# Tile 0's norm in halves, indices of eight rows first, eleven expert pieces ahead, and a new order of block sums, folds and output projections

## The chip, the cores and the metric

One core of one Trainium2 chip runs the whole program as one launch. The metric is device time in microseconds (us) from the first to the last instruction with what lies around it, as the median of the runs. Five engines work side by side, each through its own list in order: TensorE (PE, and PEld for its weight loads), VectorE (DVE), ScalarE (ACT), GpSimd (POOL) and SyncE (SP). SP and POOL also start the transfers, which share 16 DMA engines. All of the data is float32.

## The reference

256 tokens of width 1024 go through a first block of two layers and then a second block. What bears on the change:

```python
for layer in range(DEPTH):                                    # first block, DEPTH = 2
    mod = c_act @ ada_w[layer] + ada_b[layer]
    sh1, sc1, g1, sh2, sc2, g2 = split(mod, 6)
    h = rms_norm(x, norm_mix_g[layer]) * (1.0 + sc1) + sh1
    y = mlstm_moba_mixer(h, ...) if layer == 0 else diff_attention_mixer(h, ...)   # ends in y @ w_out
    x = x + g1 * y
    h = rms_norm(x, norm_ffn_g[layer]) * (1.0 + sc2) + sh2
    x = x + g2 * peer_ffn(h, peer_wq[layer], peer_keys[layer], peer_u[layer], peer_v[layer])
# peer_ffn: 8 heads, per token and head the top 16 of two lists of 128 sub-keys, the top 16 of the
# 256 pairs, softmax gates; each picked expert e adds gate * v[e] * gelu(u[e] . h)
# second block: three kinds of attention, then 32 experts in 4 groups, two for a token
x = x + concat([out_na, out_dil, out_mem]) @ w_out
x = x + hierarchical_moe(rms_norm(x, g_ffn), w_r1, b_r1, w_r2, b_r2, w1, w3, w2)
```

## The kernel before

Tokens lie in two tiles of 128 partitions (tile 0 and tile 1). The order of each engine is written out by hand; semaphores tie the engines together.

**First layer's mixer.** Weights of 2 MB (`w_slots`) stream through a ring of four places (`ring`, places 0 to 3). Places 0 and 1 take the input projection (`in0`) and the output projection (`out0`, two halves of 512 columns: `first_out` in place 1, `second_out` in place 0); places 2 and 3 take the 20 blocks of `ada_w` (`vec`, `mix`). VectorE weighs a `vec` block by the condition (`weigh(i)`) and TensorE sums it over the partitions with one product ("block sum", `project("vec", ...)`); the four `mix` blocks TensorE multiplies itself, and two of them are folded by one more product each (`fold_blocks`). A place is free when its block is weighed or its groups are multiplied (`slot_free`). Two banks of PSUM (`gp`) take all of these groups in turn: group g waits until group g-2 was copied out, nearly always by ScalarE (`move`). The list `order` numbers the groups, and the counters `gemm_done` and `gemm_moved` count them.

**Towards the retrieval.** After the attention TensorE ends `out0` for tile 0 (L1394), turns the sub-keys (`turn_keys`), multiplies `out0` for tile 1, first half (L1102), turns the normed rows, multiplies query head 0 (`first_query(0)`, L1514) and its scores (L1542), and so on to head 4; the second half of `out0` for tile 1 comes after query 1. Meanwhile VectorE adds the residual of tile 0 and norms it over its full width (`first_residual`, `sum_of_squares`, `first_norm`), then picks the best 16 of head 0 (`topk`, stages 0 to 7; stage 6 puts out the 16 indices, `idx_ready`).

**Rows of the retrieval.** 512 gathers of 1 MB (`PICKS`, L1033 on POOL) bring, for a tile and head, one expert's u and v row to each token. Row n goes to buffer n % 8; `ROW_HOMES` says in which eighth of the ring that buffer lies (homes 0 and 1 are place 0, homes 2 and 3 place 1, and so on). The first eight gathers wait for the place to be free of its weights (`slot_free`; home 4 waits for query 4), every later one for the sum of the row eight before (`vsum`, TensorE, L1555). Of each row VectorE takes the dot product with h (L3091), ScalarE makes the weight, TensorE sums the v part. The other matrix work of both layers and the second block's tile 0 is set between these rows.

**End.** When row 509 has landed SP loads the second block's weights (`in2`, `out2`) into the four places, in the order `turns_of["last"]`, each when its two row buffers are summed (`rows_left`). After the attention come the experts: 8 quads of 4 experts, each quad in 12 pieces of 2 MB (`moe_pieces`; 8 up, 4 down). The first `AHEAD` = 10 pieces have a home before the experts begin, two of them in scattered free rows (`BITS`, pieces 8 and 9); later pieces go through six places, each when TensorE has used the piece before it (`p_used`).

## Time and profile before

| | us |
|---|---|
| median of 3 runs | 2309.93 (2307.38 to 2312.25) |
| profiled execution | 2313.35 |
| its span | 2311.6 |
| PE busy | 1791.5 (77%) |
| DVE busy | 1297.5 (56%) |
| ACT busy | 851.6 (37%) |
| POOL busy | 651.6 (28%) |

The profiled execution is 3.42 us above the median of the runs, and 1.75 us of its time lie outside its span. Views speak of the time from the span's start. A stretch's DMA share is the mean busy share of the 16 DMA engines in it; PEclk is the clock granted to TensorE, as a share of 2.4 GHz. A chain of waits is followed back from the last instruction: each piece released the one behind it, or stood before it on the same engine.

### The profile page before, as it was taken

How to read it: one execution, taken by the hardware profiler on the slowest of the kernel's cores; microseconds unless marked ns; L12 is line 12 of the kernel's file. 1: busy time of each engine (PE TensorE's matmuls, PEld its weight loads, DVE VectorE, ACT ScalarE, POOL GpSimd, SP SyncE). 2: the span in 40 equal slices, each digit the busy share in tenths (PEclk: the TensorE clock that was granted, in tenths of full speed). 3: DMA queues.
4: the chain of work that ended last, by engine and by line, in shares of the span. 5: the costliest groups of instructions: out<-in, count | busy, mean ns of one | idle time of the engine just before them, and what ended most of it. 6: DMA issues, size and time to landing. Idle time of an engine off the chain costs nothing.

```text
span 2311.6 us, 30859 instructions
## 1 busy us (share of the span) xinstructions
PE 1791.5 (77%) x11196; PEld 849.1 (37%) x11196; DVE 1297.5 (56%) x3201; ACT 851.6 (37%) x2294; POOL 651.6 (28%) x606
## 2 busy tenths in 40 slices
PE   9998877695797777588779667777779997666676
PEld 4554531161252343153336112343327552222222
DVE  4877887668757766866875868465442321111111
ACT  1324354444545544454744435444433420000000
POOL 1002344434333443433443444333322300000000
PEclk9999987697798787789979666888979998787878
DMA  9989799999999999999999999999998399999998
GB/s 376 387 340 374 286 409 421 421 419 419 398 421 421 418 421 421 421 390 421 421 421 420 421 420 420 421 417 419 418 387 290 143 387 425 430 427 430 428 428 373
DMA packets 110861, 920.48 MB, mean 398 GB/s; under 512 B 12774, under 2 KB 14852, under 8 KB 18756
## 3 DMA queue, kind: packets, MB, share of 16 engines
q0 software_dynamic: 76800, 549.70, 57.8%
q1 hardware_dynamic: 33924, 369.02, 38.6%
q8 instruction: 77, 1.26, 0.2%
q14 instruction: 60, 0.49, 0.1%
HBM read 917.57 MB, written 6.06 MB: 400 GB/s over the span
## 4 chain that ended last, share of the span: by engine, by line
DMA 45%; PE 36%; DVE 9%; ACT 6%; issue 3%; POOL 1%; DVEq 0%; SPq 0%; POOLq 0%
DMA arena<-in_peer_uv_dram,arena 25%; DMA arena<-in_moe_pieces_dram 14%; PE summed L1555 8%; DVE y_g L3091 4%; PE gp L1102 4%; PE gp L1647 3%; DMA arena<-in_w_parts_dram 3%; PE gp L1116 2%; PE gp L1964 2%; DMA mod<-in_w_parts_dram 2%; PE gp L1107 2%; PE gp L1643 2%; PE gp L1776 1%; ACT arena L2308 1%; PE gp L1527 1%
## 5 line engine op out<-in xcount | busy, mean ns | idle before, releaser
L1555 PE MATMUL summed<-arena 64*64 64x512 f32 x4096 | 690.0, 767 | 338.5 <-ACT arena L2308 314.4
L3091 DVE CUSTOM_DVE_ANT_0 y_g<-arena,h 128x1024 f32<-128x1024 f32 x512 | 627.2, 1225 | 387.1 <-DMA arena<-in_peer_uv_dram,arena 329.3
L1033 POOL DMA_INDIRECT arena<-in_peer_uv_dram,arena x512 | 585.3, 1143 | 890.3 <-PE summed L1555 808.8
L1555 PEld LDWEIGHTS summed<-arena 64*64 64x64 f32 x4096 | 135.8, 157 | 757.3 <-ACT arena L2308 658.4
L2302 ACT ACTIVATE arena<-arena 128x1 f32<-128x1 f32 x512 | 102.5, 200 | 548.6 <-DVE arena L3091 547.5
L1964 PE MATMUL gp<-arena,mod 128*32 128x512 f32 x1008 | 161.4, 778 | 98.8 <-DMA arena<-in_moe_pieces_dram 98.8
L2308 ACT ACTIVATE arena<-cst,arena 128x128 f32<-128x128 f32 x512 | 205.6, 401 | 16.8
L3483 DVE TENSOR_TENSOR mod<-mod,gp 128x512 f32<-128x512 f32 x8 | 5.5, 688 | 357.8 <-ACT mod L2617 357.8
L2305 ACT ACTIVATE arena<-arena 128x1 f32<-128x1 f32 x512 | 150.8, 294 | 16.6
L1964 PEld LDWEIGHTS gp<-arena,mod 128*32 128x32 f32 x1008 | 32.1, 127 | 220.6 <-DMA arena<-in_moe_pieces_dram 160.1
L2617 ACT ACTIVATE mod<-gp 128x512 f32<-128x512 f32 x8 | 4.8, 597 | 252.2 <-PE gp L1964 252.2
L1102 PE MATMUL gp<-arena,hT 128*128 128x512 f32 x208 | 93.0, 604 | 1.2 <-ACT y_g L2090 0.7
L2881 DVE SCALAR_TENSOR_TENSOR h<-arena,cst,h 128x512 f32<-128x512 f32 x98 | 73.9, 754 | 3.4
L2302 ACT ACT_TABLE_LOAD x54 | 69.3, 1283 | 1.0
L1939 PE MATMUL summed<-mod,h 128*128 128x128 f32 x256 | 45.5, 360 | 22.6 <-DVE mod L3478 22.4
L3029 DVE FIND_INDEX8 arena<-arena 128x8 uint32<-128x128 f32 (+1 forms) x192 | 61.8, 330 | 0.0
L3026 DVE MAX8 arena<-arena 128x8 f32<-128x128 f32 (+1 forms) x192 | 58.4, 332 | 4.1 <-ACT arena L2277 0.8
L1102 PEld LDWEIGHTS gp<-arena,hT 128*128 128x128 f32 x208 | 39.4, 193 | 52.8 <-issue 50.3
L2090 ACT ACTIVATE arena<-gp 128x512 f32<-128x512 f32 (+1 forms) x26 | 15.3, 589 | 115.9 <-PE gp L1116 40.2
L2013 PE MATMUL scores<-arena,mod 128*32 128x256 f32 x984 | 56.0, 380 | 1.5 <-DMA arena<-in_moe_pieces_dram 0.8
L1116 PE MATMUL gp<-hT,arena 128*128 128x256 f32 x256 | 56.3, 380 | 0.7 <-ACT hT L2102 0.7
L1647 PE MATMUL gp<-hT,mod 128*128 128x128 f32 x416 | 49.9, 278 | 5.2 <-DMA mod<-in_w_parts_dram 5.2
(521 smaller groups left out, 2333.8 us busy)
## 6 DMA issues: line engine op xcount, KB each, us to landing
arena<-in_moe_pieces_dram SPq DMA_DIRECT2D x93, 2048.0 KB, 25.5
arena<-in_w_slots_dram SPq DMA_DIRECT2D x43, 2048.0 KB, 11.7
arena<-in_w_parts_dram SPq DMA_DIRECT2D x42, 1024.0 KB, 9.4
mod<-in_w_parts_dram SPq DMA_DIRECT2D x23, 1024.0 KB, 9.5
arena<-in_peer_uv_dram,arena POOLq DMA_INDIRECT x512, 15.5
t_rep<-t_rows POOLq DMA_DIRECT2D x1, 3066.0 KB, 18.1
arena<-t_rep POOLq DMA_DIRECT2D x1, 2304.0 KB, 12.7
ext<-in_w_parts_dram SPq DMA_DIRECT2D x2, 1024.0 KB, 16.1
```

The costliest lines, as they stand in the source:

```text
L1033: pool.indirect_dma_start(rowbuf[b], None, a["peer_uv"].rearrange("l n d -> (l n) d"), bass.IndirectOffsetOnAxis(ap=idx[:, col(n):col(n) + ...
L1102: mm = pe.matmul(bank, hT[:, k, grp[1] * P:(grp[1] + 1) * P], w[:, k, :], start=k == 0, stop=k == KT - 1)
L1116: mm = pe.matmul(bank[:, c * S:(c + 1) * S], w[:, k, grp[1] + c * P:grp[1] + (c + 1) * P], hT[:, k, :], start=k == 0, stop=k == KT - 1)
L1555: mm = pe.matmul(op[o:o + HALF, b, :], diag[i:i + HALF, n % DIAGS, i:i + HALF], rowbuf[n % ROWS][i:i + HALF, D + b * 512:D + (b + 1) * 512 ...
L1647: mm = pe.matmul(bank[:, c * P:(c + 1) * P], w[k][:, c * P:(c + 1) * P], hT[:, k, tok], start=k == 0, stop=k == KT - 1)
L1964: mm = pe.matmul(gp[c, j, :], xe[:, 2 * kk + k, c], w[:, e, k, :], start=kk + k == 0, stop=kk == 3 and k == 1, skip_group_check=True)
L2302: link(act.activation(coef[:, c:c + 1], dots[:, c:c + 1], ACT.Gelu))
L2305: link(act.activation(coef[:, c:c + 1], coef[:, c:c + 1], ACT.Copy, scale=gate[:, c:c + 1]))
L2308: act.activation(diag[:, n % DIAGS, :], ident, ACT.Copy, scale=coef[:, c:c + 1]).then_inc(diag_ready, 1)
L2881: ins = v.scalar_tensor_tensor(out=acc, in0=w[:, k, :], scalar=cact[:, k:k + 1], in1=acc, op0=ALU.mult, op1=ALU.add)
L3029: ins = v.max_index(w[:, part], b[:, part], s)
L3091: v.tensor_tensor_reduce(y[:, t, :], rowbuf[n % ROWS][:, 0:D], h[:, t, :], 1.0, 0.0, ALU.mult, ALU.add, dots[:, c:c + 1]).then_inc(udot, 1)
```

## The change

- **Halves.** `first_residual_half(b)` adds tile 0's residual by halves of 512 columns straight out of PSUM (it takes over the two copies that ScalarE made), and takes the squares by halves; `first_norm(0)` writes h by halves, and TensorE turns each half as it comes (`turn_normed`).
- **One factor row.** `scale_norm_rows` multiplies (1 + sc2) into the norm's weight row once, during the mLSTM; `first_norm` then has two passes instead of three, for both tiles.
- **Early indices.** `first_topk` puts out head 0's indices in two parts of eight; POOL waits for the first part at row 0 and for the second at row 8.
- **TensorE's order.** Block sums 8 to 11 and the two folds move from the input projection, the mLSTM and the attention to behind `turn_keys`; the first half of `out0` for tile 1 moves behind query 0's scores, block sum 17 behind query 1, and the second half stands behind query 1's scores. ScalarE's copies move with them. Weighed blocks 8 to 11 and mix parts 6 and 7 now lie in `ext`.
- **Loads.** Query heads 2 and 3 (1 MB each), of which a part lies in `ext`, load when query 0 is multiplied. Head 4 still loads when block 18 is weighed, whose last three steps now stand behind `first_topk`.
- **Homes.** `ROW_HOMES` begins with homes 0 and 1, and `turns_of["last"]` with place 0.
- **Eleven pieces ahead.** Piece 10 of the first quad gets a home: 3584 of 4096 columns in `ext`, loaded behind the last `out2` weights, and 512 columns in `gvec` and `cst`, loaded where the late parts of piece 9 are.

```diff
-ROW_HOMES = (5, 2, 3, 0, 1, 6, 7, 4)
+ROW_HOMES = (0, 1, 2, 3, 5, 6, 7, 4)
-AHEAD = 10
+AHEAD = 11
-VEC_PARTS = ((0, 0), (0, 2), (2, 3), (3, 5), (5, 6), (6, 8), (8, 10), (10, 12))
+VEC_PARTS = ((0, 0), (0, 2), (2, 3), (3, 5), (5, 6), (6, 8), (8, 8), (8, 12))
-        turns_of = dict(..., last=(1, 0, 3, 2, 0, 3, 2, 0, 3, 2))
+        turns_of = dict(..., last=(0, 1, 3, 2, 1, 3, 2, 1, 3, 2))
-        order += [(mix_slots[0], 0)] + [(n, 0) for n in vec_slots[10:12]] + [(n, 0) for n in mix_slots[1:]]
-        order += [(n, 1) for n in mix_slots[2:]]
+        order += [(n, 0) for n in mix_slots]
         first_out, second_out = phase_slots["out0"]
-        order += [(first_out, 0), (second_out, 0), (first_out, 1)]
-        order += [("query", 0), (vec_slots[16], 0), (vec_slots[17], 0), ("query", 1), (second_out, 1), ("query", 2)]
+        order += [(first_out, 0), (second_out, 0)]
+        order += [(n, 0) for n in vec_slots[8:12]] + [(n, 1) for n in mix_slots[2:]]
+        order += [("query", 0), (vec_slots[16], 0), (first_out, 1), ("query", 1), (vec_slots[17], 0), (second_out, 1), ("query", 2)]
...
+                10: (ext[:, 0:14 * S], gvec[:, 0:2 * P], cst[:, C_ROUTE:C_ROUTE + S])}
...
             load_query(1)
-            load_query(2)
...
-            load_query(3)
             for n in range(vec_slots[18], phase_slots["in2"][0]):
                 load_weights(n)
+            sync.wait_ge(gemm_done, group_of["query", 0])
+            load_query(2)
+            load_query(3)
             slot_free(sync, vec_slots[18])
             load_query(4)
...
+            first_bits(10, (0,))
             for n in range(2):
                 sync.wait_ge(gemm_done, group_end(last_held[n]))
                 first_piece(n)
...
             first_bits(9, (1, 2))
+            first_bits(10, (1, 2))
...
-                if n % TOPK == 0:
-                    pool.wait_ge(idx_ready, n // TOPK + 1)
+                if n % TOPK == 0 or n == TOPK // 2:
+                    pool.wait_ge(idx_ready, -(-n // TOPK) + 1 + (n >= TOPK))
...
+            def first_residual_half(b):
...
+                v.tensor_tensor(y[:, 0, c], modrow(2)[:, c], gp[:, g % 2, :], ALU.mult).then_inc(gemm_moved, 1)
+                v.wait_ge(gemm_moved, g + 1)
+                ins = v.tensor_tensor(x[:, 0, c], x[:, 0, c], y[:, 0, c], ALU.add)
...
+                link(v.tensor_tensor_reduce(h[:, 0, c], x[:, 0, c], x[:, 0, c], 1.0, 0.0, ALU.mult, ALU.add, s))
...
+            def scale_norm_rows():
...
+                link(v.scalar_tensor_tensor(out=gvec[:], in0=modrow(4), scalar=1.0, in1=gvec[:], op0=ALU.add, op1=ALU.mult))
...
+            def first_topk():
+
+                for stage in range(3):
+                    topk(0, 0, 0, stage)
+                for r in range(2):
+                    part = slice(8 * r, 8 * r + 8)
+                    if r:
+                        topk(0, 0, 0, 3)
...
+                    pair_rows(part)
+                    pair_hot(part)
+                    pair_index(0, 0, part)
...
-            weigh(17)
-            first_residual(0)
-            sum_of_squares(0)
+            weigh(17, 0, 5)
+            for b in range(2):
+                first_residual_half(b)
...
             first_norm(0)
-            weigh(18)
-            for stage in range(7):
-                topk(0, 0, 0, stage)
+            weigh(17, 5, KT)
+            weigh(18, 0, 5)
+            first_topk()
+            weigh(18, 5, KT)
             weigh(19)
```

TensorE from the end of `out0` for tile 0 to query 2 (rows say line, operation, out<-in, size of the out, count). Before:

```order
L1394 MATMUL gp<-arena,hT 128x512 x8
L1501 MATMUL scores<-cst,arena 128x128 x2
L1102 MATMUL gp<-arena,hT 128x512 x8
L1147 MATMUL turned<-cst,h 128x128 x8
L1514 MATMUL gp<-hT,mod 128x128 x16
L1099 MATMUL gp<-h,ones 128x512
L1542 MATMUL scores<-arena 128x128 x2
L1099 MATMUL gp<-h,ones 128x512
L1514 MATMUL gp<-hT,arena 128x128 x16
L1102 MATMUL gp<-arena,hT 128x512 x8
L1542 MATMUL scores<-arena 128x128 x2
L1514 MATMUL gp<-hT,ext 128x128 x16
```

After:

```order
L1503 MATMUL scores<-cst,arena 128x128 x2
L1103 MATMUL gp<-ext,ones 128x512 x4
L1090 MATMUL gp<-ext,cst 1x512 x2
L1176 MATMUL turned<-cst,h 128x128 x8
L1518 MATMUL gp<-hT,mod 128x128 x16
L1103 MATMUL gp<-h,ones 128x512
L1546 MATMUL scores<-arena 128x128 x2
L1106 MATMUL gp<-arena,hT 128x512 x8
L1518 MATMUL gp<-hT,arena 128x128 x16
L1103 MATMUL gp<-h,ones 128x512
L1546 MATMUL scores<-arena 128x128 x2
L1106 MATMUL gp<-arena,hT 128x512 x8
```

Four block sums and two folds took the place of the first eight L1102 (now L1106), and both halves of that projection stand between query 0 and query 2.

POOL's first gathers with the semaphores that each waits for (`acc_done` counts weighed blocks, `gemm_done` TensorE's groups). Before:

```order
L1033 DMA arena<-in_peer_uv_dram,arena 128x2048 [waits acc_done,idx_ready]
L1033 DMA arena<-in_peer_uv_dram,arena 128x2048 [waits gemm_done] x4
L1033 DMA arena<-in_peer_uv_dram,arena 128x2048 [waits acc_done] x2
L1033 DMA arena<-in_peer_uv_dram,arena 128x2048 [waits gemm_done]
L1033 DMA arena<-in_peer_uv_dram,arena 128x2048 [waits vsum] x8
```

After:

```order
L1037 DMA arena<-in_peer_uv_dram,arena 128x2048 [waits gemm_done,idx_ready]
L1037 DMA arena<-in_peer_uv_dram,arena 128x2048 [waits gemm_done] x3
L1037 DMA arena<-in_peer_uv_dram,arena 128x2048 [waits acc_done] x3
L1037 DMA arena<-in_peer_uv_dram,arena 128x2048 [waits gemm_done]
L1037 DMA arena<-in_peer_uv_dram,arena 128x2048 [waits vsum,idx_ready]
L1037 DMA arena<-in_peer_uv_dram,arena 128x2048 [waits vsum] x7
```

Row 0's gather waited for block 18 to be weighed; now, in place 0, it waits for the last group of `second_out`, which is its tile 1 group.

SP from the second block's last weights to the first piece that waits for `p_used`. After (before, the rows with `ext` and the last `gvec` and `cst` of 256 columns are not there, and the last row has x14):

```order
L808 DMA arena<-in_w_slots_dram 128x4096 [waits gemm_done] x6
L889 DMA ext<-in_moe_pieces_dram 128x3584
L879 DMA arena<-in_moe_pieces_dram 128x4096 [waits gemm_done] x2
...
L889 DMA gvec<-in_moe_pieces_dram 128x768 [waits h_ready,y_ready,r_mm]
L889 DMA cst<-in_moe_pieces_dram 128x768
L889 DMA gvec<-in_moe_pieces_dram 128x256
L889 DMA cst<-in_moe_pieces_dram 128x256
L883 DMA arena<-in_moe_pieces_dram 128x4096 [waits p_used] x13
```

Piece 10's largest part stands ahead of all other pieces and waits for nothing of its own; one piece fewer waits for `p_used`.

## Rows read from the trace of the kernel before

**Rows 1.** The page: span, busy DMA in 40 slices, and the chain by engine.

```profile
span 2311.6 us, 30859 instructions
...
DMA  9989799999999999999999999999998399999998
...
DMA 45%; PE 36%; DVE 9%; ACT 6%; issue 3%; POOL 1%; DVEq 0%; SPq 0%; POOLq 0%
```

**Rows 2.** Stretches: length, busy time by engine, then PEclk, DMA share, GB/s.

```profile
229.00:249.00 20.00, 18.49 (x104) 13.13 (x105) 18.23 (x51) 5.69 (x12) 1.70 (x2) 1.00 0.17 59
249.00:270.00 21.00, 16.84 (x134) 13.23 (x136) 19.36 (x58) 8.72 (x27) 8.96 (x9) 0.92 0.99 394
270.00:276.00 6.00, 6.00 (x57) 3.22 (x50) 3.65 (x8) 4.22 (x9) 4.90 (x4) 1.00 0.91 285
314.00:322.00 8.00, 6.81 (x54) 2.58 (x46) 7.58 (x22) 2.91 (x11) 5.59 (x6) 1.00 0.94 333
322.00:1702.00 1380.00, 1032.74 (x6416) 453.33 (x6412) 941.37 (x2287) 643.71 (x1835) 551.82 (x484) 0.82 1.01 418
1800.00:1833.00 33.00, 29.59 (x226) 19.46 (x224) 14.07 (x76) 21.73 (x52) 17.80 (x18) 1.00 0.01 2
1876.00:1882.00 6.00, 6.00 (x60) 2.04 (x62) 0.16 (x1) 1.88 (x2) 0.00 (x0) 1.00 0.52 165
1882.00:2302.00 420.00, 291.53 (x2300) 118.71 (x2292) 49.43 (x152) 28.90 (x49) 0.00 (x0) 0.83 1.01 428
266.00:268.00 2.00, 2.00 (x12) 0.55 (x12) 1.51 (x7) 1.84 (x8) 0.00 (x0) 0.50 1.01 426
```

**Rows 3.** Chain of waits, 130 to 200 us: start, us, what.

```profile
155.69 1.91 PE gp L1099 x4
...
163.41 10.86 DMA arena<-in_w_slots_dram
...
192.43 0.59 ACT ada_rows L2090
```

**Rows 4.** Chain of waits, 213 to 268 us.

```profile
213.24 7.08 PE gp L1394 x16
...
223.49 1.23 DVE h L3144
...
227.06 1.24 DVE h L3018
...
231.43 3.84 PE gp L1514 x32
235.27 0.86 PE gp L1099 x2
236.13 0.46 PE scores L1542 x4
...
241.42 6.87 PE gp L1102 x16
...
265.75 2.03 PE summed L1555 x8
```

**Rows 5.** VectorE in order of time: start, us, engine, line, what, [idle before].

```profile
177.87 0.42 DVE L2936 TENSOR_TENSOR arena<-cst,turned 128x256 f32<-128x256 f32 x1 [4.65 <-PE turned L1461]
...
246.25 0.17 DVE L3075 TENSOR_TENSOR arena<-arena 128x16 uint32<-128x16 f32 x1
```

**Rows 6.** POOL in order of time: the gathers of rows 0, 7 and 8.

```profile
247.00 1.51 POOL L1033 DMA_INDIRECT arena<-in_peer_uv_dram,arena  x1 [31.05 <-DVE arena L3075]
...
262.09 0.94 POOL L1033 DMA_INDIRECT arena<-in_peer_uv_dram,arena  x1 [5.21 <-PE gp L1514]
268.04 1.59 POOL L1033 DMA_INDIRECT arena<-in_peer_uv_dram,arena  x1 [5.01 <-PE summed L1555]
```

**Rows 7.** First quad: SP's first pieces after p_used; TensorE in its last two pieces.

```profile
1878.19 2.04 SPq L881 DMA_DIRECT2D arena<-in_moe_pieces_dram  x2
...
1904.79 3.64 PE L2013 MATMUL scores<-arena,mod 128*32 128x256 f32 x64
```

More of the change, by code:

```diff
@@ L881, in next_piece @@
                 sync.dma_start(moe_slot[r], piece_src(q, n)).then_inc(p_in[r], 16)
-            for n in range(2):
-                sync.wait_ge(gemm_done, group_end(last_held[n]))
-                first_piece(n)
             def first_bits(n, part):
@@ L891, in first_bits @@
                     c += bit.shape[1]
+            first_bits(10, (0,))
+            for n in range(2):
+                sync.wait_ge(gemm_done, group_end(last_held[n]))
+                first_piece(n)
             sync.wait_ge(y_ready, 2)
@@ L1403, in causal_attention @@
                 causal_scores(1)
-                fold_blocks()
                 causal_plain(6)
@@ L1513, in first_query @@
                     for k in range(KT):
+                        if head == 0 and c == 0 and k in (0, KT // 2):
+                            pe.wait_ge(turn_moved, turned[0] - (k == 0))
                         mm = pe.matmul(gp[:, g % 2, c * P:(c + 1) * P], w[k][:, c * P:(c + 1) * P], hT[:, k, 0:P], start=k == 0, stop=k == KT - 1)
@@ L1842, in _ @@
             turn_keys(0)
-            project("out0", slice(0, 1), tile=1)
-            pe.wait_ge(h_ready, T + 1)
-            turn_rows(h[:, 0, :])
-            hT_ready()
+            project("vec", slice(8, 12))
+            fold_blocks()
+            turn_normed(0, T)
             first_query(0)
@@ L1850, in _ @@
             score_part(0, 0, 0)
+            project("out0", slice(0, 1), tile=1)
+            first_query(1)
             project("vec", slice(13, 14))
-            first_query(1)
+            score_part(0, 0, 1)
             project("out0", slice(1, 2), tile=1)
-            score_part(0, 0, 1)
             first_query(2)
@@ L2207, in causal_attention @@
                 act.activation(small[:, 32:40], small[:, 24:32], ACT.Sqrt).then_inc(hn_rt, 1)
-                for k in (2, 3):
-                    move("mix", slice(k, k + 1), tile=1)
                 causal_moved(0)
@@ L2544, in _ @@
             causal_attention()
-            move("out0", tile=0)
+            tile_root(0)
             move_keys(0)
-            tile_root(0)
-            move("out0", slice(0, 1), tile=1)
+            act.wait_ge(gemm_moved, group_of[second_out, 0] + 1)
+            move("vec", slice(8, 12))
+            for k in (2, 3):
+                move("mix", slice(k, k + 1), tile=1)
             move_turned_rows(0)
@@ L2551, in _ @@
             move_scores(0, 0, 0)
-            move("vec", slice(12, 14))
+            move("vec", slice(12, 13))
+            move("out0", slice(0, 1), tile=1)
             move_query(0, 1)
@@ L2555, in _ @@
             act.activation(small[:, 42:44], small[:, 40:42], ACT.Exp).then_inc(lam_e, 1)
+            move("vec", slice(13, 14))
+            move_scores(0, 0, 1)
             move("out0", slice(1, 2), tile=1)
-            move_scores(0, 0, 1)
             move_query(0, 2)
@@ L2969, in mlstm @@
                 log_weights(2)
-                v.wait_ge(gemm_done, group_end(vec_slots[11]))
                 divide(0)
                 weights(2)
+                scale_norm_rows()
                 log_weights(3)
@@ L3008, in first_residual @@
                 v.wait_ge(x_ready, t + 1)
+            def first_residual_half(b):
+                n = phase_slots["out0"][b]
+                g = group_of[n, 0]
+                c = slice(b * CH, (b + 1) * CH)
+                v.wait_ge(gemm_moved, g)
+                v.wait_ge(gemm_done, g + 1)
+                v.tensor_tensor(y[:, 0, c], modrow(2)[:, c], gp[:, g % 2, :], ALU.mult).then_inc(gemm_moved, 1)
+                v.wait_ge(gemm_moved, g + 1)
+                ins = v.tensor_tensor(x[:, 0, c], x[:, 0, c], y[:, 0, c], ALU.add)
+                if b:
+                    ins.then_inc(x_ready, 1)
+                    v.wait_ge(x_ready, 1)
+                else:
+                    link(ins)
+                s = small[:, 20:21] if b else small[:, 23:24]
+                link(v.tensor_tensor_reduce(h[:, 0, c], x[:, 0, c], x[:, 0, c], 1.0, 0.0, ALU.mult, ALU.add, s))
+                if b:
+                    v.scalar_tensor_tensor(out=s, in0=s, scalar=1.0 / D, in1=small[:, 23:24], op0=ALU.mult,
+                                           op1=ALU.add).then_inc(d_sumsq, 1)
+                else:
+                    link(v.tensor_scalar(s, s, 1.0 / D, EPS, ALU.mult, ALU.add))
@@ L3017, in first_norm @@
-                v.wait_ge(gvec_used, T + t + 1)
-                link(v.scalar_tensor_tensor(out=h[:, t, :], in0=modrow(4), scalar=1.0, in1=h[:, t, :],
-                                            op0=ALU.add, op1=ALU.mult))
-                v.tensor_tensor(h[:, t, :], h[:, t, :], modrow(3), ALU.add).then_inc(h_ready, 1)
+                halves = (slice(0, CH), slice(CH, D)) if t == 0 else (slice(0, D),)
+                for c in halves:
+                    ins = v.scalar_tensor_tensor(out=h[:, t, c], in0=x[:, t, c], scalar=small[:, 22:23], in1=gvec[:, c],
+                                                 op0=ALU.mult, op1=ALU.mult)
+                    if c.stop == D:
+                        ins.then_inc(gvec_used, 1)
+                        v.wait_ge(gvec_used, T + t + 1)
+                    else:
+                        link(ins)
+                    v.tensor_tensor(h[:, t, c], h[:, t, c], modrow(3)[:, c], ALU.add).then_inc(h_ready, 1)
```

72 lines of the change are left out of this document (38 added, 34 removed).

## The prediction

> **What bounds the kernel now.** I read the page first, then stretches of the span, then the chain of waits. The page shows TensorE busy 77% of the time, but its row of busy DMA stands at 7 to 9 tenths nearly everywhere, and DMA holds the largest share of the chain, 45% [rows 1]. The stretches say it sharply: from 322 to 1702 us, where the gathers of the retrieval run, the DMA share is 1.01 at 418 GB/s, and from 1882 to 2302 us, the experts, 1.01 at 428 GB/s [rows 2]. In both a step of an engine that becomes shorter gives nothing; only fewer bytes do, or an earlier start. There are three holes: 229 to 249 us (share 0.17), 1800 to 1833 (0.01) and 1876 to 1882 (0.52) [rows 2]. So two questions decide: when does the stream of gathers start, and how many bytes are left for the experts' stage?
>
> **Eleven pieces ahead.** A piece is 128 x 4096 float32 = 2.097 MB, at 428 GB/s 4.9 us. Piece 10 goes out of the saturated stage: its large part (1.8 MB) loads ahead of the others, beside the empty stretch 1800 to 1833, and the last 0.26 MB (0.6 us) beside the 0.52 stretch [rows 2]. But the first six pieces on `p_used` are released early, from 1878.19 on [rows 7]; their data takes 6 x 4.9 = 29.4 us, to about 1909. The seventh waited for the eleventh piece to be used and now waits for the twelfth, whose product begins at 1904.79 and takes 3.64 [rows 7], so it is released at 1908.4; with about 2 us until data flows (first release 1878.19, data from about 1880 in the half-busy stretch) this leaves a hole of 0.9 us. Gain: 4.9 - 0.9 = **4.0**. Bounds: 3.3 (the late part collides with the first `p_used` pieces as well) to 4.9 (no hole).
>
> **The start of the gathers.** I follow TensorE, since in the changed order the first gather waits for one of its groups.
>
> Ahead of it the chain shows two block sums of 1.91 us at 155.69 and a copy of 0.59 us of a fold at 192.43, and it loses a second such copy [rows 3]. The 1.91 is not worth its length: 6 us later stands a 10.86 us wait for a weight load [rows 3], which is set by bytes, so I let 0.5 pass, and the copies 0.9. Gain 1.4, bounds 0 (all taken up by loads) and 1.91 + 2 x 0.59 = 3.1. `out0` for tile 0 ended at 213.24 + 7.08 = 220.32 [rows 4], now at 218.9.
>
> Of VectorE's passes, 1.23 to 1.24 us each [rows 4], halves take about 0.65. Behind the last half of `out0` stand its product, sum and squares, with small steps 2.4 us: 221.3, where the squares ended at 224.72. From there to the second norm pass (227.06) lay 2.34 us with one full pass in it, so 1.1 for root and reciprocal [rows 4]; then two halves of two passes: h at 223.7 and 225.0, before about 229.5 (227.06 and two passes).
>
> Now TensorE is in the way. Four block sums and two folds stand ahead of the transposes, in two banks, each behind a ScalarE copy of 0.59 [rows 3]; ScalarE comes to them at about 222.0, after the root and the keys. The last fold goes behind the fourth copy (222.0 + 4 x 0.63 = 224.5) and ends at 225.4; transposes and copies bring query 0 to **226.7**, against 231.43 [rows 4]: 4.7 earlier.
>
> But the first row now lies in place 0, and its gather waits for the second half of `out0` of tile 1. From query 0 to there: twice (3.84 + 0.86 + 0.46 + 6.87) = 24.06 [rows 4], so **250.8**. Before, that projection needed one product less ahead of it and ended after 241.42 + 6.87 = 248.29 [rows 4], and the gather did not wait for it at all: it went at 247.00, straight behind the indices of 246.25 + 0.17 [rows 5, 6]. The first gather comes at 251.0, **4.0 later**, though its eight indices are there by about 239.6 (scores 4.7 earlier, and about 2 us of the list's end cut off). The first row sum, 17.46 us behind that projection (265.75 against 248.29 [rows 4]), comes near 268, and the ninth gather, 2.3 behind it (268.04 [rows 6]), near 270.5; by then the first eight (19.6 us of data) have just drained, so the holes that stood at 270 to 276 (9% of 6 us) and 314 to 322 (6% of 8 us) [rows 2], together 1.0, should close. Loss: 4.0 - 1.0 = **3.0**. Bounds: 0.5 (upstream gain whole, 1.7 more, and 0.8 more of idle share caught up, from the 8% missing in row 0.92 of 249 to 270 at 394 GB/s) to 4.7 (4.0 + 1.4 with no upstream gain, less 0.7 of closed holes).
>
> **Edits with no cost.** Heads 2 and 3 (2 MB, 5.0 us of data) now load from about 230.7 in the 229 to 249 hole [rows 2] and are wanted at 250.8; if that cover were gone, each microsecond of lateness would move query 2 by one. Head 4 follows when block 18 is weighed, near 246, and is wanted near 260 (row 7's gather at 262.09 waited for its product [rows 6]). `scale_norm_rows` (one pass, 1.24) falls into VectorE's idle 4.65 us at 177.87 [rows 5]. Tile 1's norm is a pass shorter, inside a stage that the gathers bound. The new order of places in `last` lets one load start about 1 us otherwise, behind the last gathers, ahead of the hole at 1800.
>
> **Sum.** -4.0 + 3.0 = -1.0. The profiled execution of 2313.35 becomes 2312.4; it is 3.42 above the median, so the median 2309.93 becomes **2309.0**. A change of 0.2% (4.6 us) is about what a measurement of this kernel can tell from none: the forecast is "same".
>
> **Rivals.**
>
> *Faster (0.28).* The front costs nothing. TensorE reaches the end of the second half with the whole upstream gain (250.8 - 1.7 = 249.1), the gather is 2.3 us later than before, and the stream makes up 1.0 plus what it lost ahead of 270 (the 249 to 270 stretch stands at 394 against 428 GB/s: 8% of 21 us = 1.7 us [rows 2]), since eight buffers can then be filled back to back. Front 4.0 - 1.7 - 1.0 - 1.7 = -0.4; with the whole piece worth 4.9 the sum is -5.3: 2304.6. For it speaks that nothing but TensorE stands ahead of the gathers any more; against it, that the 10.86 us load is on the chain [rows 3].
>
> *Slower (0.15).* TensorE falls to its lower level in the alternation ahead of query 0. That it can is in the rows: from 266 to 268, when it has just begun the first row sum behind a wait (265.75 [rows 4]), it ran at 0.50, which is 1.2 GHz [rows 2]. Sums of 0.86 us between copies would put such waits ahead of query 0; query 0, a sum, scores and the first half of `out0` are 3.84 + 0.86 + 0.46 + 6.87 = 12.0 us of work [rows 4], doubled at that level: the gather comes 12 later, 2309.0 + 12 = 2321. It decides from 5.6 us of work at the lower level on (2309.0 + 5.6 = 2314.6, above 0.2%). Against it: the clock stood at 1.00 through 229 to 249 [rows 2], in spite of waits of TensorE for VectorE and ScalarE in the chain just ahead. The Trainium skill, "TensorE: Matmul & The Clock Gate", section "A second HAM failure mode: psum-queue depth-cycling", says that a kernel which cycles through PSUM banks lets TensorE idle a little between groups, so that its clock swings between the levels; two banks behind single copies are that pattern. By that rule this rival would be likely; the 1.00 of this trace, with the same two banks, speaks against it.
>
> *The piece brings nothing (0.10).* If the hole after the six early pieces is as long as the piece (the twelfth use is late, or the late 0.26 MB part holds SP's queue ahead of `p_used` pieces), only the front is left: 2309.93 + 3.0 = 2313. Against it: both the release and the data are worked out from rows with 1 us to spare.
>
> *It does not do what it says*: the early indices start no gather early. That is within the forecast already, since place 0 holds the gather.
>
> **How the numbers follow.** Forecast 0.47 (2307 to 2311.5), faster 0.28, piece worthless 0.10, slower 0.15. Part of the faster rival (0.04) ends within 0.2%, and part of the forecast's lower bounds (0.03) below it. Faster 0.27, same 0.58, slower 0.15. The range takes in the bounds, -4.9 + 0.5 and the faster rival's 2304.6 with 1.6 to spare, since the three runs of before alone lie 2.5 below to 2.3 above their median; on the other side 3.0 to 4.7 with no piece (2312.9 to 2314.6): 2303.0 to 2314.5.
>
> **What would show it.** Right: query 0 near 226.7; the first gather near 251, released by the last matmul of `out0` and not by VectorE; the DMA share of 240 to 250 below 0.3; first row sum near 268; the last gather 3 us later than before; the experts' stage one piece (4 to 5 us) shorter with a small hole near 1909. Wrong: the last gather lands at the same time or earlier (front overestimated), PEclk below 1.00 between 222 and 251 (slower rival), a hole of several us near 1909 or a late start of the experts (piece).

## The result and the profile after

| | before | after |
|---|---|---|
| median | 2309.16 us (2306.28 to 2313.78, 16 runs) | 2314.21 us (2307.43 to 2328.11, 16 runs) |
| ratio to before | | 1.0027 (95%: 1.0016 to 1.0037) |
| profiled execution, its span | 2313.35, 2311.6 | 2314.20, 2312.4 |

The change makes the kernel 0.27% slower. The prediction was 2309.0, "same". The medians differ by 5 us, the two profiled executions by less than 1: that of before lies 4.2 above its median, that of after on its own. And the runs of after spread over 20.7 us, where those of before spread over 7.5. Neither could be read from one trace, and both belong to the cause.

The stretches of after (length, busy time of PE, PEld, DVE, ACT and POOL, then PEclk, DMA share, GB/s), which answer to [rows 2] (the first has no counterpart there):

```profile
211.00:229.00 18.00, 16.01 (x69) 8.48 (x68) 16.45 (x32) 5.36 (x11) 0.08 (x1) 1.00 0.47 180
229.00:249.00 20.00, 20.00 (x85) 11.87 (x84) 17.93 (x59) 4.89 (x9) 0.00 (x0) 1.00 0.48 193
249.00:270.00 21.00, 16.83 (x124) 12.63 (x126) 13.83 (x48) 7.65 (x23) 10.10 (x10) 0.85 0.89 350
270.00:276.00 6.00, 4.35 (x37) 0.99 (x29) 5.86 (x12) 3.10 (x8) 4.33 (x5) 0.96 1.01 422
322.00:1702.00 1380.00, 1042.44 (x6408) 455.60 (x6408) 940.30 (x2287) 643.71 (x1834) 563.54 (x484) 0.81 1.01 417
1876.00:1882.00 6.00, 5.86 (x48) 4.29 (x50) 3.40 (x16) 1.79 (x3) 0.00 (x0) 1.00 0.82 324
1882.00:2302.00 420.00, 286.32 (x2320) 118.71 (x2316) 49.27 (x152) 29.57 (x49) 0.00 (x0) 0.85 1.00 425
```

The bound is as it was: DMA at 1.01 through the rows and 1.00 through the experts. The hole ahead of the rows is half filled (0.48 against 0.17, the query heads), 249 to 270 lost a tenth (0.89 against 0.99), and 270 to 276 is full (1.01 against 0.91), as forecast.

The chain of waits of after (start, us, what), from query 0 to the third query, beside [rows 4]:

```profile
224.29 3.81 PE gp L1518 x32
...
229.41 6.87 PE gp L1106 x16
236.27 3.57 PE gp L1518 x32
...
241.15 6.87 PE gp L1106 x16
248.02 3.58 PE gp L1518 x32
```

POOL in order of time: the gathers of rows 0, 7 and 8 in after, beside [rows 6]:

```profile
249.09 1.52 POOL L1037 DMA_INDIRECT arena<-in_peer_uv_dram,arena  x1 [38.02 <-issue]
...
261.38 0.94 POOL L1037 DMA_INDIRECT arena<-in_peer_uv_dram,arena  x1 [2.96 <-PE gp L1518]
267.83 0.94 POOL L1037 DMA_INDIRECT arena<-in_peer_uv_dram,arena  x1 [5.51 <-PE summed L1559]
```

The first gather stands 1.07 us behind the end of `out0` for tile 1 (241.15 + 6.87 = 248.02), and no longer behind the indices. The first product of the experts comes at 1880.87, 431.5 us before the end of the span; before it was 1876.28 and 435.3. So between these two executions the experts give 3.8 back, and 4.6 are lost ahead of them. The last gather of all goes 1.6 later than before:

```profile
1692.05 1.25 POOL L1033 DMA_INDIRECT arena<-in_peer_uv_dram,arena  x1 [1.53 <-PE summed L1555]
```

in before, and in after

```profile
1693.61 0.94 POOL L1037 DMA_INDIRECT arena<-in_peer_uv_dram,arena  x1 [0.38 <-PE summed L1559]
```

The other 3.0 are lost behind it. VectorE's longest wait in the second block's first attention, by the list of waits, was in after

```profile
DVE mod L2764 <- DMA mod<-na_rep: 7.7, 1, 7.7
```

and in before

```profile
DVE mod L2760 <- DMA mod<-na_rep: 0.7, 1, 0.7
```

That transfer (the bias of the neighbourhood attention, 16 loads on POOL's queue) ends while piece 10's large part, issued at 1771.40, is on the way. So a collision was the first theory. In the twelve profiles of the experiments below this wait is 1.4 to 3.6 us, and from the last gather to the experts' first product it takes 181.6 to 185.9 us, against 187.3 in after. What made the wait 7.7 in this one execution stays open.

### The profile page after: what moved, and what is told of

Read it like the earlier page. It is cut to its first block, busy times and chain, and to the rows that moved or that the text cites. A ratio compares the mean times of both kernels' runs of the same rounds, so it can differ in the third digit from the quotient of the medians.

```text
span 2312.4 us, 30876 instructions
## 1 busy us (share of the span) xinstructions
PE 1790.3 (77%) x11196; PEld 849.1 (37%) x11196; DVE 1297.3 (56%) x3217; ACT 850.9 (37%) x2292; POOL 663.3 (29%) x606
## 4 chain that ended last, share of the span: by engine, by line
DMA 48%; PE 29%; DVE 11%; ACT 6%; issue 4%; POOL 2%; SPq 0%; DVEq 0%; POOLq 0%
DMA arena<-in_peer_uv_dram,arena 26%; DMA arena<-in_moe_pieces_dram 14%; PE summed L1559 8%; DVE y_g L3153 4%; PE gp L1651 3%; DMA arena<-in_w_parts_dram 3%; DMA arena<-in_w_slots_dram 3%; PE gp L1968 2%; PE gp L1106 2%; DMA mod<-in_w_parts_dram 2%; PE gp L1647 1%; PE gp L1780 1%; ACT arena L2308 1%; PE gp L1531 1%; POOL arena L1037 1%
## 5 line engine op out<-in xcount | busy, mean ns | idle before, releaser
L1559 PE MATMUL summed<-arena 64*64 64x512 f32 x4096 | 698.5, 777 | 332.8 <-ACT arena L2308 308.3
L1037 POOL DMA_INDIRECT arena<-in_peer_uv_dram,arena x512 | 597.0, 1166 | 884.7 <-PE summed L1559 798.8
L1968 PE MATMUL gp<-arena,mod 128*32 128x512 f32 x1008 | 153.3, 744 | 104.1 <-DMA arena<-in_moe_pieces_dram 104.1
L1106 PE MATMUL gp<-arena,hT 128*128 128x512 f32 x208 | 92.0, 598 | 0.5 <-DVE hT L2757 0.5
L1106 PEld LDWEIGHTS gp<-arena,hT 128*128 128x128 f32 x208 | 39.1, 192 | 51.4 <-issue 49.6
L1120 PE MATMUL gp<-hT,arena 128*128 128x256 f32 x256 | 56.2, 380 | 1.4 <-ACT hT L2106 1.4
L2885 DVE SCALAR_TENSOR_TENSOR h<-arena,cst,h 128x512 f32<-128x512 f32 x70 | 52.9, 755 | 2.4
## 6 DMA issues: line engine op xcount, KB each, us to landing
t_rep<-t_rows POOLq DMA_DIRECT2D x1, 3066.0 KB, 17.9
```

Of the source, the lines that this page charges most:

```text
L1037: pool.indirect_dma_start(rowbuf[b], None, a["peer_uv"].rearrange("l n d -> (l n) d"), bass.IndirectOffsetOnAxis(ap=idx[:, col(n):col(n) + ...
L1106: mm = pe.matmul(bank, hT[:, k, grp[1] * P:(grp[1] + 1) * P], w[:, k, :], start=k == 0, stop=k == KT - 1)
L1120: mm = pe.matmul(bank[:, c * S:(c + 1) * S], w[:, k, grp[1] + c * P:grp[1] + (c + 1) * P], hT[:, k, :], start=k == 0, stop=k == KT - 1)
L1559: mm = pe.matmul(op[o:o + HALF, b, :], diag[i:i + HALF, n % DIAGS, i:i + HALF], rowbuf[n % ROWS][i:i + HALF, D + b * 512:D + (b + 1) * 512 ...
L1968: mm = pe.matmul(gp[c, j, :], xe[:, 2 * kk + k, c], w[:, e, k, :], start=kk + k == 0, stop=kk == 3 and k == 1, skip_group_check=True)
```

## The experiments

Each group of rows was run on one chip with the kernel before beside it: after; e1 to e4; e5 to e7; e8 to e11; e12. The medians of before there were 2309.16, 2308.67, 2310.04, 2308.86 and 2309.34, so rows of different groups are compared by their ratios. A ratio is worked out from all of the runs and need not be that of the medians. "Experts" is the span less the start of the experts' first product, from the profiled execution; rows 0 and 8 are the starts of their gathers there.

| kernel | median (range, runs) | ratio to before (95%) | row 0, row 8 | experts |
|---|---|---|---|---|
| after | 2314.21 (2307.43 to 2328.11, 16) | 1.0027 (1.0016 to 1.0037) | 249.09, 267.83 | 431.5 |
| e1 large part of piece 10 later | 2316.53 (2309.93 to 2327.98, 12) | 1.0036 (1.0021 to 1.0050) | 264.70, 282.54 | 431.8 |
| e2 ten ahead | 2321.53 (2311.76 to 2328.44, 7) | 1.0054 (1.0035 to 1.0072) | 251.52, 269.37 | 435.3 |
| e3 rows 0, 1 in place 1 | 2311.24 (2304.24 to 2323.95, 12) | 1.0017 (1.0000 to 1.0035) | 240.07, 270.48 | 430.9 |
| e4 before + piece 10 | 2306.18 (2302.76 to 2311.61, 11) | 0.9981 (0.9971 to 0.9992) | 243.14, 263.93 | 431.4 |
| e5 sums back | 2311.02 (2307.33 to 2313.96, 11) | 1.0004 (0.9995 to 1.0013) | 250.79, 268.63 | 432.1 |
| e6 e5 + e3 | 2307.39 (2304.60 to 2312.79, 11) | 0.9994 (0.9985 to 1.0003) | 236.13, 265.80 | 430.2 |
| e7 filler | 2314.43 (2309.46 to 2317.36, 11) | 1.0019 (1.0010 to 1.0028) | 252.69, 271.43 | 430.5 |
| e8 e6 + first half ahead | 2304.54 (2303.69 to 2308.73, 11) | 0.9983 (0.9974 to 0.9993) | 239.57, 266.34 | 431.6 |
| e9 two sums late | 2308.73 (2306.53 to 2315.89, 11) | 1.0004 (0.9992 to 1.0016) | 247.10, 265.83 | 430.9 |
| e10 e6 with ten ahead | 2314.71 (2308.04 to 2316.46, 9) | 1.0023 (1.0013 to 1.0033) | 239.68, 270.09 | 436.7 |
| e11 e4 again | 2305.11 (2301.49 to 2307.03, 11) | 0.9982 (0.9973 to 0.9991) | 243.68, 264.73 | 430.5 |
| e12 e8 + block 18 ahead | 2303.81 (2300.67 to 2306.75, 9) | 0.9975 (0.9965 to 0.9985) | 237.40, 261.01 | 430.5 |

One more execution of e2 took 7253.51 us, three times any other; there is no trace of it, and it is left out of its row's median and range.

**First series: is it piece 10, or the rest?** e1 issues the large part behind the first two whole pieces:

```diff
-            first_bits(10, (0,))
             for n in range(2):
                 sync.wait_ge(gemm_done, group_end(last_held[n]))
                 first_piece(n)
+            first_bits(10, (0,))
```

> The changed kernel, with piece 10's large part (1.8 MB into ext) issued behind the first two whole pieces instead of ahead of them, so near 1798 us, in the empty stretch, instead of at 1771. Theory 1 (collision): the part, issued at 1771.40, shares the DMA engines with the last neighbourhood-bias transfers (mod<-na_rep), for which VectorE waited 7.7 us instead of 0.7; then this kernel keeps the gain of the experts' stage (3.8) and loses the 4.5 of the stretch 1712 to 1838: about 2305.5, runs within some 8 us of each other, bias wait under 2 us. Theory 2 (places and front): the third batch of bias transfers was issued 5.9 us later already before 1771 (1760.45 against 1754.59), so the new order of places, or the shifted rows, is at fault; then nothing changes: about 2314, bias wait several us.

e2 sets `AHEAD = 10` in the changed kernel and takes out piece 10's loads.

> The changed kernel without piece 10 ahead (ten ahead as before). Theory 1 (collision with piece 10's large part): the bias wait falls under 2 us and the experts' stage is as long as before (about 435 us from its first product to the end), so 2309.2 + 0.2 of the front = 2309.4, with the narrow spread of before. Theory 2 (places and front): the 4.5 us stay and the 3.8 are lost too, about 2318.

e3 puts the places back:

```diff
-ROW_HOMES = (0, 1, 2, 3, 5, 6, 7, 4)
+ROW_HOMES = (2, 3, 0, 1, 5, 6, 7, 4)
-        turns_of = dict(..., last=(0, 1, 3, 2, 1, 3, 2, 1, 3, 2))
+        turns_of = dict(..., last=(1, 0, 3, 2, 0, 3, 2, 0, 3, 2))
```

> The changed kernel with rows 0 and 1 in place 1 (homes 2, 3, 0, 1, 5, 6, 7, 4) and the places of the last weights in the order of before. Front: the first two gathers no longer wait for the second half of out0 of tile 1 and go near 237 to 238, released by the early indices or by the first half. If the start of the gathers bounds the stream, the last row lands up to 4 us earlier (two rows of 1 MB at about 2.4 us each); if the ninth gather, behind the first row sum near 265, bounds it, the landing stays at 1712. Theory 1 (collision): the bias wait and the wide spread stay, 2310 to 2314. Theory 2 (places): the bias wait falls under 2 us, 2306 to 2309.

e4 is the kernel before with `AHEAD = 11`, piece 10's home and its loads, and nothing else.

> The kernel before with eleven pieces ahead and nothing else of the change, the large part of piece 10 issued ahead of the other pieces as in the changed kernel. Theory 1 (collision): the bias wait grows to several us, the experts' stage is 3.8 us shorter, runs spread over 15 us or more as those of the changed kernel, median 2310 to 2314. Theory 2 (places and front): bias wait under 2 us, 2305.4.

e3's first two gathers go 9 us earlier than after's, as expected, but its ninth does not (270.48, with a front that begins 2.65 later, 210.95 against 208.30 at the last part of `out0` for tile 0), and the last goes with after's (1693.12): two early rows alone do not start the stream earlier. The collision fell as an account of the medians: with the part issued late the bias wait is 1.6 us and the time no better; without the part the wait is 2.4 us and the time is worse; in the kernel before the same piece at the same place gains 0.19% and the runs stay together. (Theory 2 had the wait stay at several us, and that failed too.) The slow executions lose their time in the front. The profiled one of e1, 2327.98 us, shows it: its first gather goes at 264.70, 15.6 later than in after, with the same code ahead of it. TensorE in order of time in e1, around the second and third `mix` block in the mLSTM (L1080; in brackets the idle time before, and what ended it):

```profile
159.85 0.73 PE L1490 MATMUL summed<-ones,arena 128*128 128x1 f32 x6
164.22 3.64 PE L1080 MATMUL gp<-arena,cst 128*32 128x512 f32 x16 [3.64 <-DMA arena<-in_w_slots_dram]
...
174.71 3.64 PE L1080 MATMUL gp<-arena,cst 128*32 128x512 f32 x16
...
194.51 0.93 PE L1346 MATMUL scores<-arena 64*128 64x128 f32 x8
```

The block takes 3.64 us instead of 1.92, behind an idle time of 3.64 us, and so does the next, which waited for nothing. Stretches of e1:

```profile
160.00:165.00 5.00, 1.36 (x11) 0.70 (x13) 2.21 (x2) 0.47 (x2) 0.00 (x0) 0.80 1.01 419
165.00:170.00 5.00, 5.00 (x19) 0.94 (x12) 0.00 (x0) 0.26 (x1) 0.00 (x0) 0.50 0.37 157
170.00:190.00 20.00, 20.00 (x72) 9.64 (x71) 7.34 (x25) 2.54 (x6) 0.00 (x0) 0.50 0.98 401
```

TensorE is busy through 165 to 190 and has 1.2 GHz. In after the same place reads:

```profile
160.00:165.00 5.00, 3.02 (x16) 0.59 (x16) 1.23 (x2) 0.00 (x0) 0.00 (x0) 0.66 0.99 406
165.00:170.00 5.00, 5.00 (x36) 2.86 (x36) 2.72 (x10) 1.40 (x3) 0.00 (x0) 1.00 0.82 279
170.00:190.00 20.00, 18.25 (x118) 10.66 (x112) 15.66 (x52) 10.27 (x22) 6.24 (x7) 0.91 1.01 429
```

Here the wait was 2.39 us, the block took 3.24, and the clock fell too (0.66) but was back in the next stretch. The 0.91 behind it is a second fall, at the place that the folds left. In after TensorE waits there for VectorE, and the products behind the wait take 2.93 us:

```profile
185.22 2.93 PE L1368 MATMUL turned<-cst 128*128 128x128 f32 x12 [1.04 <-DVE arena L2725]
```

In before a fold stands there, and they take 1.60:

```profile
189.59 1.03 PE L1086 MATMUL gp<-h,cst 128*1 128x512 f32 x4
190.70 1.60 PE L1364 MATMUL turned<-cst 128*128 128x128 f32 x12
```

In before two of the sums that the change moved away stand in the wait for the second `mix` block (163.31, L1099). TensorE waits 0.28 us there, and 1.91 ahead of the third block:

```profile
163.31 1.98 PE L1099 MATMUL gp<-h,ones 128*128 128x512 f32 x4
...
166.80 1.92 PE L1076 MATMUL gp<-arena,cst 128*32 128x512 f32 x16 [0.28 <-DMA arena<-in_w_slots_dram]
...
174.31 1.92 PE L1076 MATMUL gp<-arena,cst 128*32 128x512 f32 x16 [1.91 <-DMA arena<-in_w_slots_dram]
```

The waits of the four executions with all four sums moved are 2.39 (after), 3.64 (e1) and 3.79 (e3), each with a fall, and 1.86 (e2), without one.

The Trainium skill, "TensorE: Matmul & The Clock Gate", section "HAM oscillation — how this bites in real kernels", describes this for a product with few rows: the wait for the next load between two bursts lets the clock fall, and the burst behind it starts at the lower level. The rows of e1 agree: 0.50 behind the wait.

What a fall costs shows in the length of this stage, from the last product ahead of the mLSTM (L1215; sums 8 and 9 follow it where they are in place) to the last part of `out0` for tile 0 (L1398). In after:

```profile
150.93 1.05 PE L1215 MATMUL summed<-arena,cst 128*32 128x512 f32 x4
208.30 7.13 PE L1398 MATMUL gp<-arena,hT 128*128 128x512 f32 x16
```

and in e5, which has the sums and folds back (below):

```profile
153.90 1.05 PE L1215 MATMUL summed<-arena,cst 128*32 128x512 f32 x4
210.24 7.13 PE L1398 MATMUL gp<-arena,hT 128*128 128x512 f32 x16
```

That is 57.37 and 56.34 us. All seven experiments with the sums and folds in place have 56.2 to 56.5; the profiled execution of before, with its late load, has 58.53. With all six moved it is 57.37 (after), 72.15 (e1) and 59.01 (e3), each with a fall, and 56.44 (e2), without one. So 5 us of TensorE's work (1.98 + 1.98 + 1.03) left this stage, and it became shorter in none of the four executions; a fall makes it 1 to 16 us longer.

**Second series: the sums.** e5 undoes one part of the change:

```diff
                         if hh == 0:
                             mix(0)
+                            project("vec", slice(10, 12))
...
                 causal_scores(1)
+                fold_blocks()
...
             turn_keys(0)
-            project("vec", slice(8, 12))
-            fold_blocks()
```

with the list of groups, ScalarE's copies and `VEC_PARTS` to match.

> The changed kernel with block sums 8 to 11 and the two folds at the places of before (two sums behind the input projection, two in the mLSTM, the folds in the attention), all else changed. Theory A (clock): in the changed kernel TensorE stands idle for 2.4 to 3.8 us ahead of the second mix block because the sums no longer fill that wait, and its clock falls to 0.50 there, for a length that differs from run to run (first gather 249.09 in one run, 264.70 in another). Then here the clock stays 1.00 from 150 to 210, the first gather goes at 246 to 248, the runs lie within 10 us of each other and the median is 2306 to 2309. Theory B (the rows' places and the order of the out projection alone cost the time): spread and median of the changed kernel stay, 2312 to 2316.

e6 is that, with e3's places.

> As the run with the sums put back, and rows 0 and 1 in place 1, so that the first gather waits for the early indices alone. Theory A: clock 1.00, narrow spread; the first two gathers near 236 to 238, two rows of 1 MB (2.4 us each) move into the hole ahead of 249. If the start of the gathers bounds the stream of rows, 3 to 5 us below the run with the sums put back, so 2302 to 2305; if the ninth gather, behind the first row sum, bounds it, no difference, 2306 to 2309. Theory B: 2308 to 2312, with the wide spread.

e7 leaves the change as it is and adds products that nothing reads:

```diff
             def mix(k):
+                if k == 1:
+                    g = group_of[mix_slots[1], 0]
+                    pe.wait_ge(gemm_moved, g - 1)
+                    for _ in range(5):
+                        pe.matmul(gp[:, g % 2, :], ident, cst[:, 0:CH], start=True, stop=True)
                 project("mix", slice(k, k + 1), tile=0)
```

> The changed kernel with five products of 128x512 that nothing reads, ahead of the second mix block in the mLSTM (about 4.5 us of TensorE at full clock, in the wait for that block's weights). They are of no use to the result: only TensorE's activity changes. Theory A (clock): the clock stays 1.00 from 150 to 200, spread within 10 us, median 2307 to 2310 although work was added; the first gather at 249 to 251. Theory B: nothing changes or up to 2 us are added, 2314 to 2316 with the wide spread.

Both keep TensorE busy at the place, e5 with work that has to be done and e7 with none, and in both the clock stays up. Stretches of e5:

```profile
160.00:165.00 5.00, 5.00 (x28) 1.87 (x21) 3.82 (x2) 2.08 (x5) 0.00 (x0) 1.00 1.01 372
165.00:170.00 5.00, 5.00 (x33) 2.33 (x33) 1.26 (x5) 1.66 (x5) 0.00 (x0) 1.00 1.03 387
```

Stretches of e7:

```profile
160.00:165.00 5.00, 5.00 (x33) 2.41 (x26) 4.20 (x3) 2.06 (x5) 0.00 (x0) 1.00 1.00 387
165.00:170.00 5.00, 5.00 (x24) 1.56 (x22) 0.03 (x1) 0.00 (x0) 0.00 (x0) 1.00 0.87 351
```

The spread falls from 20.7 us to 6.6 (e5) and 7.9 (e7); no run of either is above 2318, where 5 of 16 of after are. In the profile of e7 the stage measured above takes 56.22 us again. So the spread is shown to come from TensorE's clock in the mLSTM.

For the median less is shown. With the six products back (e5) the kernel is 0.23% or 5 us faster (1.0004 against 1.0027, intervals apart), so moving them costs that much. How much of it is the clock stays open: e7 keeps the clock up without moving the products back, and its median stays at 2314, where 2307 to 2310 was expected. Its ratio (1.0019) lies within after's interval, and its interval just overlaps that of e5. Its five products took 4.54 us in a wait of 2.4 to 3.8, and its profiled execution reached the mLSTM late (at 156.66, in after at 151.92).

The rival that no run separates is the products' new place, where query 0 stands behind them. In after it begins 16.0 us behind the start of the last part of `out0` for tile 0 (208.30 to 224.29); in e9 below, with two sums there and no folds, 14.1 us (208.26 to 222.31). And e5 has a fall of its own: nothing fills the wait for VectorE ahead of the transposes now, the clock has a mean of 0.56 from 220 to 226, and query 0 takes 5.10 us instead of 3.81:

```profile
222.40 1.11 PE L1176 MATMUL turned<-cst,h 128*128 128x128 f32 x4 [3.24 <-DVE h L3057]
...
224.70 5.10 PE L1520 MATMUL gp<-hT,mod 128*128 128x128 f32 x32
```

Its median (2311.02) and its first gather (250.79) miss what theory A expected (2306 to 2309, and 246 to 248).

**Third series: what is left.** e8 puts the first half of `out0` for tile 1 ahead of the transposes again:

```diff
+            project("out0", slice(0, 1), tile=1)
             turn_normed(0, T)
             first_query(0)
             project("vec", slice(12, 13))
             pe.wait_ge(keys_m, 1)
             score_part(0, 0, 0)
-            project("out0", slice(0, 1), tile=1)
```

> As the run with the sums put back and rows 0 and 1 in place 1, and the first half of out0 for tile 1 ahead of the transposes again, as in the kernel before. TensorE stands idle there for 3.2 to 3.5 us while VectorE norms tile 0. Theory F (where the projection stands delays the first row sum): query 4 ends and the ninth gather goes 4 to 6 us earlier than 265.8, near 260 to 262, and the time falls by 3 to 5 us against the run without this edit, to 2302 to 2304. Rival: the stream of rows is paced by later things (weights of the first rows, VectorE), and the time falls by under 1.5 us.

e9 puts back sums 8 and 9 and the folds, and leaves 10 and 11 behind `turn_keys`.

> The changed kernel with block sums 8 and 9 and the folds at the places of before; only sums 10 and 11 are moved out of the mLSTM, behind the turned keys. Theory A (TensorE's clock falls in the wait for the second mix block, which those two sums filled): the wide spread is back, to 2320 and over in some runs, the clock at 0.50 behind that wait in the profile if it is one of the long ones, median 2312 to 2316. Rival A2 (sums 8 and 9 or the folds matter, not those two): clock 1.00 and a narrow spread as with all sums back, 2309 to 2312.

e10 is e6 with ten pieces ahead.

> As the run with the sums put back and rows 0 and 1 in place 1, but with ten pieces ahead: the price of piece 10 between two kernels with a narrow spread. By the prediction's term 4.0 us slower than with eleven (bounds 3.3 to 4.9), so 2310.7 to 2312.3. Rival (the large part of the piece collides with the bias transfers and gives half of it back): 1 to 2 us slower, 2308.5 to 2309.5.

e11 is e4 once more.

> The kernel before with eleven pieces ahead, a second time, beside the other three on one chip: 3 to 4.5 us under the kernel before again if the piece is worth its term of 4.0; under 2 us if the first series was luck.

e9 speaks against the narrow form of the theory: with two of the four sums back TensorE comes to that wait later, stands 1.24 us, and keeps its clock:

```profile
161.58 0.73 PE L1492 MATMUL summed<-ones,arena 128*128 128x1 f32 x6
163.55 1.92 PE L1081 MATMUL gp<-arena,cst 128*32 128x512 f32 x16 [1.24 <-DMA arena<-in_w_slots_dram]
```

Its stage takes 56.12 us, its runs spread over 9.4 us and its ratio is that of e5, so rival A2 came true: moving two of the sums does no such harm, moving all four and the folds does. e10 prices piece 10: 6.7 us by the ratios (1.0023 against 0.9994), more than the 3.3 to 4.9 expected, of which part is a later front in its profile (ninth gather 270.09 against 265.80), and 4.7 in the experts' stage, where the three profiles with ten pieces ahead have 435.3, 435.3 and 436.7 and the eleven others 430.2 to 432.1 (means 435.8 and 431.1).

e8 gains 0.11% on e6, but not as expected: the ninth gather stays at 266.34. The chain of waits of e8 says why:

```profile
245.20 9.72 DMA arena<-in_w_parts_dram
254.97 5.43 PE gp L1520 x32
```

Query head 4's weights, which the change sends when block 18 is weighed behind the indices, now run beside the first rows, take 9.72 us, and TensorE waits 2.15 us for them; behind that wait it runs at 0.50 from 255 to 258, and query 4 takes 5.43 us. Nor is e8's gain that of the projection's place alone: the projection now fills the wait ahead of the transposes, and the clock from 220 to 226 is 1.00 (0.72 in e6). e12 weighs block 18 in one piece ahead of `first_topk`:

```diff
-            weigh(18, 0, 5)
+            weigh(18)
             first_topk()
-            weigh(18, 5, KT)
```

> As the run with the sums put back, rows 0 and 1 in place 1 and the first half of the out projection ahead, and block 18 weighed in one piece ahead of the indices, so that query head 4's load goes some 13 us earlier, near 232, into the hole, instead of at 245.20 beside the first rows (it took 9.72 us there, and query 4 waited 2.15 us for it). Theory H (that load holds the first row sum): query 4 no longer waits, the ninth gather comes 2 us earlier or more than 266.34, the indices 2.3 us later, the time 1 to 3 us under the run without this edit (median 2304.54). Rival (the first rows are then bound by the later indices or by VectorE): no difference, within 1 us.

In e12's chain of waits query 4 begins at 250.72, right behind the scores of query 3:

```profile
250.01 0.71 PE scores L1548 x4
250.72 3.59 PE gp L1520 x32
```

The ninth gather goes at 261.01, 5.3 earlier than in e8, of which 2.4 are there already at the last part of `out0` for tile 0 (207.21 against 209.57). The time falls by 0.08%, within the intervals of the two (0.9983 and 0.9975), so that gain is not settled. Against before e12 stands at 0.9975 (0.9965 to 0.9985), the lowest of all, and its whole range lies below the median of before.

## Why the prediction was wrong

Step by step, as it was put:

- **What bounds the kernel**: right in the main. The gains and losses that the runs show are an earlier or later start of the rows, or bytes taken out of the experts' stage. After's own profile has 3.0 us elsewhere, between the last gather and the experts, where it waits for the bias.
- **Eleven pieces, -4.0**: right, a little small. e4 and e11 give 0.9981 and 0.9982, 4.3 us (2.5 and 3.8 by their medians); the stage is 4.7 shorter. The hole behind the six early pieces is there, at 1912 to 1914 in after, with a share of 0.82.
- **Upstream, +1.4 gained**: this is the step that failed, and in sign. I counted the removal of the sums and folds from the mLSTM and the attention as 0.5 and 0.9 us gained. The stage is not shorter without them even where the clock holds (56.44 us in e2, against 56.2 to 56.5), so the gain is nothing. Without them the wait at the second `mix` block is 1.9 to 3.8 us, the clock fell behind it in three of four executions, and that made the stage 1 to 16 us longer. Over all runs, moving them costs 0.23% (after against e5), of which the clock's part at the median stays open. Two readings led me there. I priced 10.86 us for a weight load [rows 3] as a property of the kernel; it was that execution's, which was simply a late one: its last part of `out0` for tile 0 begins at 213.24 [rows 4], that of after at 208.30, which would look like a gain beyond the upper bound, but e4 and e11, with TensorE's order of before, begin it at 207.72 and 209.87. And I took the chain's piece of DMA for idle time of TensorE. The chain names what released the next product; of these 10.86 us TensorE stood idle for 0.28 + 1.91, and among what it did were two of the sums that the change takes away.
- **The slower rival**: right in kind, wrong in place. I looked for the fall where the sums went, ahead of query 0, between ScalarE's copies; there the clock stands at 1.00 (211 to 229 and 229 to 249, above). The Trainium skill, "TensorE: Matmul & The Clock Gate", section "A second HAM failure mode: psum-queue depth-cycling", tells of a kernel whose clock swings because it cycles through PSUM banks, and by that the prediction called this rival likely. The rows do not agree: 1.00 in both stretches. The fall happens where the sums came from, and the chance of 0.15 left that place out.
- **The start of the rows, +3.0**: right in mechanism and nearly in size. Query 0 came at 224.29 for 226.7, the second half of `out0` ended 23.7 us behind that for 24.06, and the gather followed it. Against e4, whose front has the order of before and a like start, after's ninth gather is 3.9 later (267.83 against 263.93) and the last gather of all 3.7 (1693.61 against 1689.91). From e4 and e11 to e5 the ratios give 0.22%, 5 us. That step holds all else that differs between e4 and e5, too. Putting the places and the out projection's first half back gives 0.21% (e5 to e8, intervals apart); each alone, 0.10% (e5 to e6) and 0.11% (e6 to e8), is not settled, since the intervals overlap.
- **Edits with no cost**: right for after, but head 4's late load had its cover from the very delay of the rows. When the rows come earlier it is the next thing to be late (e8, e12).
- **The sum**: read as a chain of ratios, -4.3 (piece: before to e4 and e11), +5 (rows' places and the projection's order: e4 and e11 to e5), +5 (sums and folds moved: e5 to after) is about +6, which is the measured 0.27%. The forecast had the first two, the second as 3.0, and the third as a gain. That 2314.21 lies within the stated range (2303.0 to 2314.5) is luck: its upper end stood for a piece that brings nothing.
- **Halves, early indices, one factor row**: with the three harmful parts undone (e8) the kernel stands at 0.9983, where the piece alone gives 0.9981 and 0.9982. No gain of theirs can be measured there; it takes head 4's load out of their way (e12) for a hint of one.

## What to carry to other kernels

Work that gains no time where it stands may be what keeps TensorE's clock up: before moving small products out of a wait for a load, read the idle time that is left there and the clock behind it, and leave them if that wait would grow. A piece of DMA in a chain of waits is not idle time of the engine behind it; look at that engine's own list in the same stretch. And a step of one trace is one execution: where a load's landing sets it, a second execution, or the spread of the times, tells whether the wait belongs to the kernel.

## What the runs showed of the hardware

Behind one wait of 3.64 us TensorE ran at 0.50 from 165 to 190 us although it was busy in all of that time (20.00 of 20 us from 170 to 190, e1). In e3 a wait of 3.79 us at the same place slowed one block only:

```profile
164.51 3.39 PE L1080 MATMUL gp<-arena,cst 128*32 128x512 f32 x16 [3.79 <-DMA arena<-in_w_slots_dram]
167.83 1.04 PE L1084 MATMUL gp<-ada_b,cst 24*32 24x512 f32 x2
...
182.44 0.93 PE L1346 MATMUL scores<-arena 64*128 64x128 f32 x8
```

From that block to the first scores of the next attention (L1346) it is 182.44 - 164.51 = 17.9 us in e3 and 194.51 - 164.22 = 30.3 in e1. Nearly the same wait, then, can cost 12 us more or less, which is about what the spread of the changed kernel grew by (from 7.5 to 20.7 us).

The length of a wait does not tell whether the clock falls. In after it fell behind the 1.04 us ahead of L1368 (0.83 from 180 to 190). In e2 it did not behind the same 1.04 us at that place (1.00 from 186 to 192), nor in before behind 1.91 us (1.00 from 170 to 180).
